# Splitting the next feed-forward part's first two weight blocks in halves inside the mixer, with fewer filler products at the norms

## What is computed

```
for l in range(DEPTH):                                   # DEPTH = 2
    mod = c_act @ ada_w[l] + ada_b[l]                    # shifts, scales and gates of the three parts
    h = modulate(rms_norm(x, ffn1_norm[l]), sh1, sc1)
    x = x + 0.5 * g1 * swiglu(h, w_gate1, w_up1, w_down1)
    h = modulate(rms_norm(x, mix_norm[l]), sh2, sc2)
    z = h @ w_in[l]
    y = concat([pool(z), mla_attention(z)]) @ w_out[l]
    x = x + g2 * y
    h = modulate(rms_norm(x, ffn2_norm[l]), sh3, sc3)
    x = x + 0.5 * g3 * swiglu(h, w_gate2, w_up2, w_down2)
return rms_norm(x, final_norm)
```

## Time and profile before

| | us |
|---|---|
| median of 3 runs (lowest, highest) | 1282.73 (1281.85, 1286.23) |
| profiled execution, first to last instruction | 1280.1 |
| PE busy | 1258.1 (98%) |
| DVE busy | 1007.1 (79%) |
| ACT busy | 601.9 (47%) |
| POOL busy | 89.1 (7%) |

### The profile page before, as it was taken

How to read it: one execution, slowest core, us unless ns; L and a number is a source line. 1 busy time by engine, 2 the same in 40 slices (tenths; PEclk the granted TensorE clock), 3 DMA queues, 4 the chain that set the end, 5 groups by cost and what they waited for, 6 DMA issues and landing times.

```text
span 1280.1 us, 26147 instructions
## 1 busy us (share of the span) xinstructions
PE 1258.1 (98%) x11088; PEld 1228.4 (96%) x11088; DVE 1007.1 (79%) x1652; ACT 601.9 (47%) x859; POOL 89.1 (7%) x159
## 2 busy tenths in 40 slices
PE   9999999999999999999999999999999999999997
PEld 7899999998999999999999989999999987999997
DVE  4899998876888667999988867899965957766665
ACT  4544335575433635433335665333344466633333
POOL 0111110000111040111110000000001000000000
PEclk9999999999999999999999999999999999999999
DMA  9999997441888653999994424545543423455551
GB/s 369 384 397 384 376 355 287 150 147 39 326 342 323 238 200 119 346 370 355 360 379 134 162 98 150 220 175 198 200 149 117 160 75 113 180 199 190 188 191 42
DMA packets 66101, 293.89 MB, mean 230 GB/s; under 512 B 7745, under 2 KB 8897, under 8 KB 51905
## 3 DMA queue, kind: packets, MB, share of 16 engines
q1 hardware_dynamic: 47552, 225.10, 48.1%
q0 software_dynamic: 18432, 67.12, 13.1%
HBM read 291.14 MB, written 1.05 MB: 228 GB/s over the span
## 4 chain that ended last, share of the span: by engine, by line
PE 87%; DVE 6%; ACT 2%; DMA 2%; SPq 2%; issue 1%; DVEq 0%; ACTq 0%
PE gu_bank L642 16%; PE gu_bank L644 15%; PE gu_bank L643 15%; PE y_bank L642 7%; PE y_bank L644 7%; PE y_bank L643 7%; PE t_bank L642 3%; PE t_bank L644 2%; PE t_bank L643 2%; DVE dn_lo L1816 2%; PE gu_bank L629 1%; DMA raw_gu<-ffn_gu 1%; PE gu_bank L694 1%; PE gu_bank L698 1%; PE gu_bank L695 1%; SPq L469 1%
## 5 line engine op out<-in xcount | busy, mean ns | idle before, releaser
L642 PE MATMUL gu_bank<-hT_hi,gu_hi 128*128 128x256 f32 x1668 | 461.5, 277 | 3.8 <-DVE hT_lo L1802 1.6
L643 PE MATMUL gu_bank<-hT_lo,gu_hi 128*128 128x256 f32 x1668 | 460.7, 276 | 0.0
L644 PE MATMUL gu_bank<-hT_hi,gu_lo 128*128 128x256 f32 x1668 | 460.7, 276 | 0.0
L642 PEld LDWEIGHTS gu_bank<-hT_hi,gu_hi 128*128 128x128 f32 x1668 | 313.1, 188 | 5.1 <-issue 3.4
L644 PEld LDWEIGHTS gu_bank<-hT_hi,gu_lo 128*128 128x128 f32 x1668 | 313.1, 188 | 0.0
L643 PEld LDWEIGHTS gu_bank<-hT_lo,gu_hi 128*128 128x128 f32 x1668 | 313.1, 188 | 0.0
L1821 DVE TENSOR_TENSOR gu_lo<-raw_gu,gu_hi 128x2048 fp32r<-128x2048 f32 x105 | 240.8, 2293 | 39.3 <-ACT gu_hi L1326 34.1
L1326 ACT ACTIVATE gu_hi<-raw_gu 128x2048 fp32r<-128x2048 f32 x100 | 191.1, 1911 | 40.0 <-DMA raw_gu<-ffn_gu 40.0
L1343 ACT ACTIVATE sg<-gu_bank 128x256 f32<-128x256 f32 x88 | 33.8, 385 | 354.2 <-PE gu_bank L644 354.2
L642 PE MATMUL y_bank<-act_hi,dn_hi 128*128 128x256 f32 x660 | 183.2, 278 | 0.0
L643 PE MATMUL y_bank<-act_lo,dn_hi 128*128 128x256 f32 x660 | 182.3, 276 | 0.0
(11 more groups left out here) (508 smaller groups left out, 2169.5 us busy)
## 6 DMA issues: line engine op xcount, KB each, us to landing
raw_gu<-ffn_gu SPq DMA_DIRECT2D x110, 1024.0 KB, 6.3
stage<-ada POOLq DMA_DIRECT2D x128, 512.0 KB, 7.7
raw_dn<-ffn_dn SPq DMA_DIRECT2D x110, 512.0 KB, 3.7
ring<-mix_w SPq DMA_DIRECT2D x72, 512.0 KB, 3.6
stage<-ada SPq DMA_DIRECT2D x8, 512.0 KB, 14.1
pro<-ada SPq DMA_DIRECT2D x6, 512.0 KB, 12.9
x<-x_in SPq DMA_DIRECT2D x1, 1024.0 KB, 5.8
ring<-ada SPq DMA_DIRECT2D x2, 512.0 KB, 17.4
```

Of the source, the lines that this page charges most:

```text
L642: pe.matmul(to, a[0], b[0], start=start, stop=False)
L643: pe.matmul(to, a[0], b[1], start=False, stop=False)
L644: return pe.matmul(to, a[1], b[0], start=False, stop=stop)
```

## The change

In the two first-kind mixers the single split of block 0 and the two halves of block 1 become four half splits, at other places:

- ACT: block 0's gate half goes between the splits of units 19 and 20, its up half behind the first three turned heads (`pT`), block 1's gate half between the splits of units 21 and 22, its up half behind the last mixed chunk. Unit 22's split moves ahead of the last mixed chunk.
- DVE: both lo halves of block 0 go behind unit 20's lo, block 1's first behind unit 21's, then unit 22's lo, then `mixed(7)`, then block 1's second half. A new semaphore, `gu0_hi_half`, marks block 0's first half.
- PE: `busy(4)` ahead of the sums of squares behind the mixer goes. The `busy(3)` behind the rows becomes `busy(1)`, at the norm behind each of the two mixers and at the norm between layer 0 and layer 1.

```
@@ PE, main loop
                 mixer(l)
                 pe.wait_ge(tile_out, TILES * (l + 1))
-                busy(4)
                 sums(3 * l + 2)
                 busy(2)
                 rows(3 * l + 2)
-                busy(3)
+                busy(1)
                 for bank_ in gu_bank:
                     clear(bank_)
                 ffn(2 * l + 1, True)
...
                     rows(3 * l + 3)
-                    busy(3)
+                    busy(1)
@@ ACT
+            def split_half(f, b, h):
+
+                act.wait_ge(gu_loaded[b], 8 * FB * f + 16)
+                act.activation(gu_hi[:, b, h, :, :].rearrange("p c n -> p (c n)"), raw_gu[:, b, half_block(h)], ACT.Copy)\
+                   .then_inc(gu_hi_done if h else (gu0_hi_half, gu1_hi_half)[b], 1)
...
                 softmax(3)
-                for c in range(3):
+                for c in range(2):
                     split(l, SPLITS - KC + SLOTS + c)
+                split_half(2 * l + 1, 0, 0)
+                split(l, SPLITS - KC + SLOTS + 2)
                 for h in range(HEADS - 1):
                     take(ACT.Copy, pT[:, h, :], 384)
+                split_half(2 * l + 1, 0, 1)
                 mixed(POOLG)
                 take(ACT.Copy, pT[:, HEADS - 1, :], 384)
                 mixed(POOLG + 1)
                 mixed(POOLG + 2)
                 split(l, SPLITS - KC + SLOTS + 3)
+                split_half(2 * l + 1, 1, 0)
+                split(l, SPLITS - 1)
                 mixed(POOLG + HEADS - 1)
                 assert seen[0] == TILES
-                split_block0(2 * l + 1)
-                split(l, SPLITS - 1)
-                split_block1(2 * l + 1)
+                split_half(2 * l + 1, 1, 1)
                 table(ACT.Sqrt)
@@ DVE
+            def lo_half(f, b, h):
+
+                last = dve.tensor_tensor(gu_lo[:, b, h, :, :].rearrange("p c n -> p (c n)"), raw_gu[:, b, half_block(h)],
+                                         gu_hi[:, b, h, :, :].rearrange("p c n -> p (c n)").bitcast(F32), ALU.subtract)
+                if h:
+                    last.then_inc(gu_lo_done, 1)
+                elif b:
+                    last.then_inc(gu1_lo_half, 1)
+
+            def split_block0_half(f, h):
+
+                dve.wait_ge(*((gu0_hi_half, f // 2 + 1), (gu_hi_done, FB * f + 1))[h])
+                lo_half(f, 0, h)
...
                 lo(20)
+                for h in range(2):
+                    split_block0_half(2 * l + 1, h)
                 for c in range(POOLG, KC - 1):
                     mixed(c)
                 lo(21)
+                split_block1(2 * l + 1, 0)
+                lo(22)
                 mixed(KC - 1)
-                split_block0(2 * l + 1)
-                lo(22)
+                split_block1(2 * l + 1, 1)
...
                 mixer(l)
-
-                for h in range(2):
-                    split_block1(2 * l + 1, h)
                 modulation(l, 2)
```

More of the change, by code:

```diff
@@ L293, in program @@
         gu_hi_done, gu_lo_done, dn_hi_done, dn_lo_done = sem("gu_hi_done"), sem("gu_lo_done"), sem("dn_hi_done"), sem("dn_lo_done")
-        gu1_hi_half, gu1_lo_half = sem("gu1_hi_half"), sem("gu1_lo_half")
+        gu1_hi_half, gu1_lo_half, gu0_hi_half = sem("gu1_hi_half"), sem("gu1_lo_half"), sem("gu0_hi_half")
         gu_ps, silu_done, prod_done, act_hi_done, act_done, dn_used, y_ps = (
@@ L1311, in split_block0 @@
                 act.activation(gu_hi[:, 0, :, :, :].rearrange("p h c n -> p (h c n)"), raw_gu[:, 0, :], ACT.Copy).then_inc(gu_hi_done, 1)
+            def split_half(f, b, h):
+                act.wait_ge(gu_loaded[b], 8 * FB * f + 16)
+                act.activation(gu_hi[:, b, h, :, :].rearrange("p c n -> p (c n)"), raw_gu[:, b, half_block(h)], ACT.Copy)\
+                   .then_inc(gu_hi_done if h else (gu0_hi_half, gu1_hi_half)[b], 1)
             def split_block1(f):
-                act.wait_ge(gu_loaded[1], 8 * FB * f + 16)
-                for h, signal in enumerate((gu1_hi_half, gu_hi_done)):
-                    act.activation(gu_hi[:, 1, h, :, :].rearrange("p c n -> p (c n)"), raw_gu[:, 1, half_block(h)], ACT.Copy).then_inc(signal, 1)
+                for h in range(2):
+                    split_half(f, 1, h)
             def ffn(f, before_last=None, beside=lambda n: None):
@@ L1825, in split_block0 @@
                 split_gu(FB * f, 0)
+            def lo_half(f, b, h):
[8 more added lines that the diff above has]
+                lo_half(f, 0, h)
             def split_block1(f, h):
                 dve.wait_ge(*((gu1_hi_half, f + 1), (gu_hi_done, FB * f + 2))[h])
-                last = dve.tensor_tensor(gu_lo[:, 1, h, :, :].rearrange("p c n -> p (c n)"), raw_gu[:, 1, half_block(h)],
-                                         gu_hi[:, 1, h, :, :].rearrange("p c n -> p (c n)").bitcast(F32), ALU.subtract)
-                last.then_inc(gu_lo_done if h else gu1_lo_half, 1)
+                lo_half(f, 1, h)
             def ffn(f, pair, beside, before_last, between):
```

## The result

| | before | changed |
|---|---|---|
| median of 5 runs beside each other (lowest, highest), us | 1283.01 (1281.85, 1286.47) | 1269.16 (1268.67, 1271.12) |
| profiled execution: span, us | 1280.1 | 1267.5 |
| PE busy, us | 1258.1 | 1249.0 |

The ratio of the times is 0.9889, with a 95% interval of 0.9877 to 0.9900: the kernel is 1.1% faster. Put on the 1282.73 us of before, that is 1268.5 us, 14.2 us less. The forecast was 1271.8 us, 10.9 us less, with a range from 1268.8 to 1276.6. The sign, the touched places and the mechanism there came as forecast, but some 3 us of gain were missing from the sum. The rest of this document is about where they came from.

The account below looks back on a forecast made before the run. PE's own work, busy 1258.1 of 1280.1 us, plus few waits set the end. Mixer 0 6.0, norm between layers 0.44 and mixer 1 4.4 gave 10.9 us: span 1269.2, plus 2.6, median 1271.8 us; range 1268.8 to 1276.6.

Parts of the forecast that it names:

- Part 1, the half splits: Projection's end in both mixers: halves fit ACT's and DVE's holes, PE's stall goes, 2.4 us in each mixer.
- Four things that were to be seen: Projection's end: no PE wait for lo, lo done early, residual within 0.1 us of y, granted clock not below 1.0.
- Part 2, `busy(4)`: Between projection and sums: squares ready 0.5 us ahead of PE, so removing the filler gains 1.54 us in each mixer.
- the second rival: Sums in both mixers: residual and squares end last, up to 1.0 us of 1.54 lost each; 1273.8 us, chance 0.09.
- Part 3, `busy(3)` to `busy(1)`: Next part's start at three norms: 0.44 us each, limited by the first hi chunk; 1.3 us together.
- Part 4, the clock in mixer 0: Projection behind mixer 0's stall: the half clock goes with the stall, 1.6 us; 0 to 3.2 us for both mixers.
- the sum over places: Mixer 0 6.0, norm between the layers 0.44, mixer 1 4.4 us; together 10.9 us, nothing counted elsewhere.
- none for `mixed(7)`: Projection's end: rival that the stall moves to PE waiting for the last mixed chunk; at worst 1278.2 us, chance 0.07.
- no drop at a norm: The three norms: first rival, that fewer fillers let the clock drop, 1.6 us each, 1276.6 us for three; chance 0.12.
- the long half clock: Behind each norm: rival that PE stays at 1.2 GHz, 12 us each giving 1289 us, slower than before; chance 0.04.

Follow-up runs that it names:

- before again: The kernel before, unedited, run and traced a second time: 1282.53 us against 1282.20 us, ratio 1.0003.
- splits alone: The changed kernel with the removed filler products put back, so only the half splits and new order differ from before: 1276.59 us, ratio 0.9956.
- fillers alone: The kernel before with only the filler products taken out (busy(4) gone, busy(3) to busy(1)), weight splits unmoved: 1277.22 us, ratio 0.9965.
- short start: The kernel before with 28 filler products taken out of its start and nothing else changed: 1281.91 us, ratio 0.9996.
- padded: The changed kernel with 28 small products of 16 columns put into the start: 1276.20 us, ratio 0.9947.
- lo inside the scan: The changed kernel with DVE's lo of unit 9 moved from behind the second state scan into it: 1269.23 us, ratio 0.9896.
- no filler at the last norm: The changed kernel without the busy(3) ahead of the joint sums of squares behind the first block: 1268.95 us, ratio 0.9894.
- no fillers at the norms: The changed kernel without the busy(2) and busy(1) it keeps at the same three norms: 1272.81 us, ratio 0.9923.

## Why the prediction came out as it did

**Part 1, the half splits: right.** 2.4 us were forecast per mixer. By the traces of before again and of the splits alone 2.5 and 2.4 us went there, besides the clock. Nothing waited on ACT or DVE at the moved steps. Four things that were to be seen were seen: no wait for the unit's lo, the lo done ahead of PE's asking, the residual right behind y (0.95 us of waiting for it), no window below 1.0.

**Part 2, `busy(4)`: right.** The sums start directly and end without a wait. The last two residual steps end at 755.79 and the last square at 756.24; PE would have had to wait if it had been later than about 756.5 (754.73 + 16 x 0.112). The cover was some 0.3 us where 0.5 was forecast, so the second rival was close. The fillers-alone kernel shows the other side: with the stall in place this cover is not there, and the squares take back 1.2 us of the 1.54 in mixer 0. So the two parts help each other.

**Part 3, `busy(3)` to `busy(1)`: slightly too high.** 0.44 us were forecast at each norm, and 0.30 came; PE waits 0.40 us for the first hi chunk at each of the three, so that chunk was the bound, as forecast, and came a little later than laid out. From the start of the sums to the first product it is 5.25 us, forecast 5.1, before 5.55. Another 0.19 us per mixer came unforeseen: the clearing product stands 0.11 us ahead of the sums and not 0.30 as behind a filler. The two errors cancel, which is luck.

**Part 4, the clock in mixer 0: right as a mean.** Behind the 8 stalls in the four traces of kernels that have them (before twice, the fillers alone, the short start) the clock fell 4 times, for 3.4 us each. That is one drop, or 1.6 us, per execution, as forecast. The Trainium skill, "TensorE: Matmul & The Clock Gate", Part 1, has the half clock as the default state that activity of the array releases. The traces agree: every drop in the twelve traces between the first 50 us and the last 10 follows a stall, a stop or, without fillers, two gaps of PE. The prediction called the drop in mixer 0 the only one in its rows; the same trace has a second one of 3.4 us, behind the stop at the state inputs.

**The step that failed** is the sum over places: I took what an edit of PE's list costs to lie only where the instructions stand. 56 instructions fewer ahead of the state inputs moved the borders of the instruction transfers, and a stop of about 2 us, which the trace of before showed in plain view as "issue", no longer came. The sum had that place at nothing, and it gave 2.2 us, most of the missing 3. In all twelve traces the stop goes by the length of the list:

| PE's list ahead of the state inputs | kernels | stop |
|---|---|---|
| as before | before (2 traces), splits alone, padded | 1.84 to 2.30 us after product 252 |
| 28 pairs shorter | changed (3 traces), fillers alone, short start, lo inside the scan | none |
| 34 pairs shorter | no filler at the last norm | none |
| 46 pairs shorter | no fillers at the norms | 0.16 us after product 170 |

**The second missed term** is the execution that the sum started from. The spans differ by 12.6 us and the medians by 13.85. The changed kernel's traced execution took 1269.41 us for a span of 1267.5, an offset of 1.9 us, and lay 0.25 us above its median. With the same offset the traced one of before took 1282.0 us and lay 1.0 us below its median. I carried 1282.73 - 1280.1 = 2.6 us over as if all of it lay around the span. Some of it was time at half clock that the traced execution happened not to have: it had 11.2 us of it, before's runs have 12.8 us in the median (7.7 to 20.5), worked out as (1 - mean clock) x 2 x span, and the changed kernel has 7.6 us (5.1 to 10.2), the last microseconds of the kernel included in each. Half of the difference, 0.8 us, is about what the traced execution lay below its median.

So the missing 3 us, 13.85 - 10.9 = 2.95, are 2.2 us at the state inputs, 1.25 us from the choice of the execution, 0.17 us at the touched places and 0.2 us elsewhere, less the 0.88 us that the changed kernel's traced execution lost in the start, where it had 3.4 us of half clock and the one of before had none.

**The rivals.** No wait for a square and none for `mixed(7)` came, and no drop at a norm, so none of them happened, though the run without fillers shows that the first was close by. Nor was the long half clock to be seen.

**Why the stop lasts 2 us in one place and 0.16 us in another.** The records of the instruction transfers answer this in part (us; the product is the last one ahead of the gap):

| trace | product, started | transfer | next product | behind the transfer's end |
|---|---|---|---|---|
| before | 252, 986.67 | 986.54 to 987.49 | 988.79 | 1.30 |
| before again | 252, 989.43 | 989.18 to 990.07 | 991.55 | 1.48 |
| splits alone | 252, 981.42 | 981.57 to 982.50 | 983.81 | 1.31 |
| padded | 252, 981.67 | 981.91 to 982.79 | 984.25 | 1.46 |
| no fillers at the norms | 170, 976.75 | 974.69 to 975.82 | 977.18 | 1.36 |

In each of the five, PE goes on 1.3 to 1.5 us behind the end of a transfer. In the kernels without a gap, the last transfer had ended 1.32 us or more ahead of the product behind the border (changed: 972.36, product 153 at 973.68). So the length of the stop goes by how late the transfer began. How late that is can be told by the borders that the arithmetic gives. Behind the first border in the series the changed kernel's next transfer began after 0.6 us, with the DMA engines 3% busy in the two microseconds ahead of it; without fillers at the norms it was 1.6 us at 61%. At 90% and more it was 2.9 to 4.4 us in all twelve traces. It was as late in the changed kernel as in the one before (976.77, behind product 152 at 973.59), but there the border that it serves lies behind the series, where products take longer. With a piece used up in 128 x 29 ns = 3.7 us, a start 3.5 us late, 0.9 us of transfer and 1.3 us behind it leave a gap of 2.0 us, an estimate from these rows.

**What stays open.** First, whether the data transfers make the instruction transfers late: the two go together in these traces, and no run here takes the data transfers away. The arithmetic with the borders rests on a few list lengths (a border in mid-series at other lengths left no gap), and that PE waits for instructions is inferred from it and from the times of the transfers, not seen. Second, the two parts alone give 5.6 and 5.0 us, together 14.1 us by the medians of runs beside each other. Of the surplus of 3.5 us the traces explain about 1 us (the fillers gave 4.4 us at the norms with the splits in place and 3.1 us without them); each of the three has an uncertainty of 1 to 2 us, and I leave the rest unexplained.

## What to carry to other kernels

Splitting work that isn't urgent into pieces that fit the idle holes of ACT and DVE, and putting the last urgent piece first, is worth the full wait that it ends, and then lets fillers go that were only covering a late engine; keep those that cover a real gap (of 0.4 and 0.9 us here). Read the waits marked "issue" of the busiest engine before an edit: such a stop may come or go with the number of instructions ahead of it, in either direction, so a range must hold it (here 2 us, 0.15%). And a gain in front of a stretch that another engine paces should be counted only up to that engine's lead.

## What the runs showed of the hardware

- PE can stop for 1.84 to 2.30 us with nothing to wait for by semaphore, in a dense series of short products (29 ns a pair), and whether it does depended on the number of PE instructions ahead, even where those were added or removed 900 us earlier.
- Instruction transfers are 16.4 KB each (1.44 MB / 88), one for every 126 of PE's products, and the list lengths fit one border every 128 pairs of load and product.
- In five traces with a stop PE went on 1.30 to 1.48 us behind the end of an instruction transfer. Such a transfer began 0.3 to 0.9 us behind a border where the DMA engines were up to 19% busy, and 2.9 to 4.4 us behind it where they were 90% busy or more.
- A stall of PE of 2.26 us brought the half clock in 4 of 8 cases, for 3.4 us at a cost of 1.6 us. Gaps of 0.88 and 0.83 us with short work between them brought it in one of three.
- Behind twenty-eight products of 16 columns in a row at the start, the granted clock was 0.59 and 0.56 in two windows of 4 us, and 5.2 us were lost.
